# Layer 0's output stage in another order round tile 1, with the first expert group's 16 U rows gathered and multiplied in it

## The reference, cut to what matters

```python
# end of the mLSTM mixer; hs = both scan directions, 4 heads of 256
hn = (hs - mu) * lax.rsqrt(var + NORM_EPS) * norm_w          # per head
y = (sigmoid(o) * hn) @ w_out
x = layer_norm(DEEPNORM_ALPHA * x + m[2] * y, ln_mix_g, ln_mix_b)
f = peer_ffn(modulate(x, m[3], m[4]), w_q, subkeys, u_tab, v_tab)
x = layer_norm(DEEPNORM_ALPHA * x + m[5] * f, ln_ffn_g, ln_ffn_b)

def block(xt):                                               # peer_ffn, 128 tokens
    qh = (xt @ w_q).reshape(128, 8, 2, 128)
    s = einsum('thpd,hpnd->thpn', qh, subkeys)
    v_top, i_top = top_k(s, 16)
    sc, pos = top_k(sums of the 16 x 16 pairs, 16)           # 16 experts of a head
    gate = softmax(sc)
    act = gelu(einsum('td,ted->te', xt, u_tab[eidx]))        # U row times token
    return einsum('te,ted->td', gate * act, v_tab[eidx])     # weighted sum of V rows
```

## Time and profile before

| | before |
|---|---|
| median of 3 runs | 4410.88 us |
| profiled execution: its span | 4409.3 us |
| its own time beside the span | not recorded; the span is 1.6 us below the median of the runs |
| mean granted TensorE clock | 0.931 of 2.4 GHz |
| TensorE busy | 3529.3 us, 80% |
| VectorE busy | 3058.1 us, 69% |
| ScalarE busy | 746.8 us, 17% |
| GpSimd busy | 2512.6 us, 57% |
| DMA moved | 1491.65 MB, mean 338 GB/s |
| of it the gathers (software queue) | 1342.34 MB, 77.3% of the 16 DMA engines' span |

### The profile page before, as it was taken

One profiled execution on the slowest core, in us unless ns is written; L12 is line 12 of the kernel. 1 busy time (PEld: TensorE's weight loads), 2 busy tenths in 40 slices (PEclk: granted clock), 3 DMA queues, 4 the chain that ended last, 5 costly groups with the idle time before them and its releaser, 6 DMA issues. The chain is left out here.

```text
span 4409.3 us, 41525 instructions
## 1 busy us (share of the span) xinstructions
PE 3529.3 (80%) x11702; PEld 1756.0 (40%) x11702; DVE 3058.1 (69%) x7280; ACT 746.8 (17%) x2088; POOL 2512.6 (57%) x2589
## 2 busy tenths in 40 slices
PE   5987768888888888877977675888888888788876
PEld 3456544334333434422445343333343333333332
DVE  2754578777777777776779467766676766676776
ACT  0011111111111111211024131111111111111221
POOL 0000017767677777776755103777777777777775
PEclk8988889999999999999987787999999999999999
DMA  6731329999999999999987634999999999999998
GB/s 241 252 133 19 110 83 403 405 407 407 398 404 405 399 406 404 401 404 381 371 331 246 209 115 184 408 407 405 405 404 405 401 406 405 401 404 405 402 409 345
DMA packets 453089, 1491.65 MB, mean 338 GB/s; under 512 B 49860, under 2 KB 71236, under 8 KB 452612
## 3 DMA queue, kind: packets, MB, share of 16 engines
q0 software_dynamic: 368640, 1342.34, 77.3%
q1 hardware_dynamic: 80068, 138.34, 9.3%
q10 hardware_dynamic: 4160, 8.39, 0.6%
HBM read 1484.07 MB, written 4.82 MB: 338 GB/s over the span
## 5 line engine op out<-in xcount | busy, mean ns | idle before, releaser
L1629 DVE SCALAR_TENSOR_TENSOR wrk<-wrk,ps 128x1024 f32<-128x1024 f32 x1184 | 1439.9, 1218 | 801.8 <-DMA wrk<-in_peer_u,route_gate 801.2
L1567 POOL DMA_INDIRECT wrk<-in_peer_u,route_gate x1184 | 1124.8, 950 | 729.9 <-issue 458.3
L1431 PE MATMUL ps<-mod,diag 128*128 128x512 f32 x1152 | 568.4, 618 | 153.5 <-DMA mod<-in_peer_v,route_gate 153.2
L1576 POOL DMA_INDIRECT mod<-in_peer_v,route_gate x584 | 567.7, 972 | 178.5 <-issue 158.8
L1431 PE MATMUL ps<-mod,y 128*128 128x512 f32 x1184 | 530.3, 597 | 16.8 <-DMA mod<-in_peer_v,route_gate 16.8
L1431 PE MATMUL ps<-lnw,y 128*128 128x512 f32 x592 | 343.6, 735 | 223.7 <-ACT y L1505 222.7
L1431 PEld LDWEIGHTS ps<-mod,diag 128*128 128x128 f32 x1152 | 197.6, 189 | 516.4 <-DMA mod<-in_peer_v,route_gate 369.2
L1576 POOL DMA_INDIRECT lnw<-in_peer_v,route_gate x292 | 278.1, 952 | 210.9 <-DVE route_gate L1156 121.9
L1431 PE MATMUL ps<-big,diag 128*128 128x512 f32 x576 | 285.5, 618 | 100.5 <-DMA big<-in_peer_v,route_gate 100.5
L1431 PEld LDWEIGHTS ps<-mod,y 128*128 128x128 f32 x1184 | 217.8, 191 | 279.8 <-issue 222.2
L1576 POOL DMA_INDIRECT big<-in_peer_v,route_gate x292 | 276.1, 946 | 89.1 <-issue 73.2
(11 more groups left out here) (517 smaller groups left out, 4291.7 us busy)
## 6 DMA issues: line engine op xcount, KB each, us to landing
wrk<-in_gla_w_in SPq DMA_DIRECT2D x12, 2048.0 KB, 13.1
wrk<-in_peer_u,route_gate POOLq DMA_INDIRECT x1184, 9.3
big<-in_peer_w_q SPq DMA_DIRECT2D x16, 1024.0 KB, 16.7
mod<-modulation_rows SPq DMA_DIRECT2D x22, 512.0 KB, 6.6
lnw<-in_ada_w SPq DMA_DIRECT2D x14, 768.0 KB, 6.0
mod<-in_ada_w SPq DMA_DIRECT2D x40, 256.0 KB, 3.2
qk<-in_ada_w SPq DMA_DIRECT2D x13, 768.0 KB
mod<-in_ada_w SPq DMA_DIRECT2D x13, 768.0 KB, 6.1
```

The source lines that it names most:

```text
L1431: mm = pe.matmul(m.ps[:, b + h, :], diag[r], ring_v[r % RV][:, h * HALF:(h + 1) * HALF], start=r == 0 and i % 2 == 0, stop=r == on_pe(i) - ...
L1567: pool.indirect_dma_start(ring_u[r % RU], None, u, bass.IndirectOffsetOnAxis(ap=expert_slot(m, slot_at[work[i]])[:, r:r + 1], axis=0)).the ...
L1576: pool.indirect_dma_start(ring_v[r % RV], None, v, bass.IndirectOffsetOnAxis(ap=expert_slot(m, slot_at[work[i]])[:, r:r + 1], axis=0)).the ...
L1629: dve.scalar_tensor_tensor(out=ring_u[r % RU], in0=ring_u[r % RU], scalar=1.0, in1=xm_ps, op0=ALU.mult, op1=ALU.mult, accum_out=act_u[i % ...
```

## The change

In `mixer_output`:
- Both halves of w_out are loaded before the modulation and layer norm rows. `output(0, 1)` follows `output(0, 0)` directly.
- `head_norm` writes alternately into `m.y` and `m.diag`, so it waits for the transpose of two tiles before.
- VectorE does three head norms, then tile 1's residual (straight from PSUM) and `prepare`, head norm 3, the routing of group 0, head norm 4, then 16 dots of group 0 with the 14 pieces of group 1's routing between them, and last the four other residuals. TensorE does tile 1's queries and scores as soon as it can, in the middle of `output(1, 1)`.
- The other four products are copied by ScalarE from PSUM to `wrk` rows (`keep`), and their residuals read them there.
- GpSimd gathers the 16 U rows of group 0 in this stage, into a ring of 6 buffers (`Lead`).

In `peer`, layer 0: no U rows and dots of group 0. VectorE prepares the four tiles and starts `period(0)`. GpSimd starts with V rows of group 0 and U rows of group 1 in turn. In both layers: the V ring has 9 rows (five early ones, `big` 12, 13, 14, 5 and `wrk` 13, and four of `mod`), the second layer norm's rows go to `lnw`, and the scaling of X by ALPHA is done by ScalarE (`scale_tile`, five multiplications behind `copy_xT(4)`). `late` is an empty list in both layers, so what hangs on it does nothing.

```diff
@@ mixer_output @@
+    y = [m.y[:], m.diag[:]]
...
-            sp.dma_start(W[:, :, 0:HALF], w[:, :, 0:HALF]).then_inc(w_loaded[0], 16)
+            for n in range(2):
+                sp.dma_start(W[:, :, n * HALF:(n + 1) * HALF], w[:, :, n * HALF:(n + 1) * HALF]).then_inc(w_loaded[n], 16)
             load_rows(sp, m, a, layer, 0, (2,), "mix", loaded)
-            sp.dma_start(W[:, :, HALF:D], w[:, :, HALF:D]).then_inc(w_loaded[1], 16)
...
+        @block.gpsimd
+        def _(pool):
+            pool.wait_ge(head.sem, head.at(3, "gated"))
+            pool.sem_inc(lead.gather_passed, 1)
+            pool.wait_ge(front.route.sem, front.route.at(0, "expert"))
+            lead.gather(pool, u)
...
+            def keep(k):
+                act.wait_ge(product, k + 1)
+                act.copy(product_row(m, order[k]), pair_at(out_bank[k % 2])).then_inc(kept, 1)
...
+            front.copy_queries(act)
             front.copy_scores(act, 0)
             front.copy_scores(act, 1)
+            lead.show(act, front.act_scores)
+            keep(1)
             front.exp(act, 0)
+            evacuate(3)
+            sqrt_head(4)
+            keep(2)
             evacuate(4)
             front.exp(act, 1)
+            keep(3)
+            layer_norm_sqrt(act, m, rest, rest_act, 1)
+            layer_norm_sqrt(act, m, rest, rest_act, 2)
+            keep(4)
...
-                if k > 0:
-                    dve.wait_ge(transposed, k)
+                if k > 1:
+                    dve.wait_ge(transposed, k - 1)
...
+            head_norm(3)
+            for k in range(14):
+                front.route_piece(dve, passed, 0, k)
             head_norm(4)
-            front.routes(dve, passed)
-            residual(3)
-            residual(4)
+            pieces = route_one()
+            for r in range(TOPK):
+                lead.dot(dve, passed, r)
+                next(pieces, None)
+            for k in range(1, N):
+                dve.wait_ge(kept, k)
+                if k > 1:
+                    dve.wait_ge(rest.sem, rest.at(k - 1, "done"))
+                for _ in residual_steps(dve, m, rest, rest_act, k, order[k], product_row(m, order[k]), passed):
+                    pass
@@ peer @@
-    ring_v = [m.lnw[:, 0], m.lnw[:, 1], row_of(m.big, 14), row_of(m.big, 5)] + \
-             [m.mod[:, n, c, :] for n in range(2) for c in range(2)]
+    v_early = [row_of(m.big, 12), row_of(m.big, 13), row_of(m.big, 14), row_of(m.big, 5), row_of(m.wrk, 13)]
+    v_more = [m.mod[:, n, c, :] for n in range(2) for c in range(2)]
+    V_OPENS = len(late) * TOPK if late else len(v_early)
...
+            for n in range(2 if late else NT):
+                scale_tile(n)
...
             def row_u(i, r):
-                if i >= 1 or r >= RU:
+                if (i - U0) * TOPK + r >= RU:
                     pool.wait_ge(used_u, i * TOPK + r + 1 - RU)
...
             routed(0)
+            if lead:
+                routed(1)
+                for r in range(len(v_early)):
+                    row_v(0, r)
+                    row_u(1, r)
+                for r in range(len(v_early), RU):
+                    row_u(1, r)
+                for r in range(len(v_early), TOPK):
+                    row_v(0, r)
+                    if r + RU - len(v_early) < TOPK:
+                        row_u(1, r + RU - len(v_early))
...
-                if r >= 4 and r % 2 == 0 and r < 4 + 2 * NT:
...
-                    dve.tensor_scalar(m.X[:, t, :], m.X[:, t, :], ALPHA, None, ALU.mult).then_inc(summed, 1)
```

More of the change, by code:

```diff
@@ L10 @@
 from contextlib import ExitStack
+from itertools import chain
 import numpy as np
@@ L997, in _ @@
+            layer_norm(dve, m, rest, rest_act, 0, z, m.X[:, 1, :], "added", passed)
             dve.wait_ge(rest.sem, rest.at(0, "done"))
             front.prepare(dve)
-            head_norm(2)
-            residual(1)
             head_norm(3)
-            residual(2)
+            for k in range(14):
+                front.route_piece(dve, passed, 0, k)
             head_norm(4)
-            front.routes(dve, passed)
-            residual(3)
-            residual(4)
-def load_rows(sp, m, a, layer, first, which, ln, sem, rows=None):
+            pieces = route_one()
@@ L1011, in load_rows @@
+            for r in range(TOPK):
+                lead.dot(dve, passed, r)
[5 more added lines that the diff above has]
+                for _ in residual_steps(dve, m, rest, rest_act, k, order[k], product_row(m, order[k]), passed):
+                    pass
+def load_rows(sp, m, a, layer, first, which, ln, sem):
     for n in which:
@@ L1262, in routes, with __init__, peer @@
             for k in range(14):
-                routing_step(dve, self.m, self.b, self.layer, self.route, self.act_scores, self.act_exp, passed, R, R, k)
-def peer(nc, m, a, layer):
+                self.route_piece(dve, passed, R, k)
+class Ring:
+    def __init__(self, early, more, opens, total):
+        self.rows = early + more
+        free, self.slot, self.landing, self.after = list(range(len(early))), [], [], []
+        times, user = [0] * len(self.rows), [None] * len(self.rows)
+        for g in range(total):
+            if g == opens:
+                free = list(range(len(early), len(self.rows))) + free
+            n = free.pop(0)
+            free.append(n)
+            times[n] += 1
+            self.slot.append(n)
+            self.landing.append(times[n] * 16)
+            self.after.append(user[n])
+            user[n] = g
+def peer(nc, m, a, layer, lead=None):
     RU = RV = 8
+    U0 = 1 if lead else 0
     HALF_ROWS = TOPK // 2
@@ L1354, in _ @@
         def _(sp):
-            load_rows(sp, m, a, layer, 3, (2,), "ffn", rows_in, ln_rows)
+            for c in (1, 0):
+                if late:
+                    sp.wait_ge(rest.sem, rest.at(1 if c else 2, "scaled"))
+                sp.dma_start(m.mod[:, 2, c, :], a["rows"][layer, c, 5 * D:6 * D].partition_broadcast(P))\
+                    .then_inc(gate_in[c], 16)
+            if late:
+                sp.wait_ge(rest.sem, rest.at(len(late) - 1, "done"))
+            for n, name in enumerate(("g", "b")):
+                sp.dma_start(m.lnw[:, n, :], a[f"ln_ffn_{name}"][layer].partition_broadcast(P)).then_inc(ln_in, 16)
             for n in range(1, EH // 2):
@@ L1514, in group @@
                     layer_norm_sqrt(act, m, fin, fin_act, finished.index(tile(i - 2)))
+                if late and i == 0:
+                    copy_queries(2)
+                    copy_scores(2)
+                    layer_norm_sqrt(act, m, rest, rest_act, 0)
                 if len(now) == 2:
@@ L1693, in modulate_next, with route_steps, late_steps @@
                 dve.tensor_tensor(y, y, next_mod[0], ALU.add).then_inc(next_ready, 1)
+            def route_steps(R, first=0):
+                for k in range(first, 14):
+                    route_piece(R, k)
+                    yield
+            def late_steps(j):
+                t = late[j]
+                if j > 0:
+                    dve.wait_ge(rest.sem, rest.at(j - 1, "done"))
+                yield from residual_steps(dve, m, rest, rest_act, j, t, product_row(m, t), passed)
+                prepare(order.index(t))
+                yield
             def period(i):
```

342 lines of the change are left out of this document (203 added, 139 removed).

## The result

| | before | after |
|---|---|---|
| median (lowest to highest, runs) | 4410.43 us (4408.67 to 4413.34, 4) | 4387.49 us (4385.79 to 4388.14, 4) |
| ratio, 95% interval | | 0.9946 [0.9932, 0.996] |
| span of the profiled execution | 4409.3 us | 4385.7 us |
| mean granted clock | 0.931 | 0.933 |

The changed kernel is 22.9 us faster; 4391 was forecast. A second session with other executions gave 4392.3 us (4390.85 to 4394.56, 5 runs), ratio 0.9961 [0.9947, 0.9975] (`again_after`). First the head of its page, with busy time by engine and the GB/s of the 40 slices.

A forecast was written before the change was run, and what follows sets the result against it. DMA bound the expert stage's steady part, while VectorE ended the output stage with DMA share 0.26. Output stage +2.9, expert start -22, layer 1 -1.2 make -20.3: span 4409.3 becomes 4389.0, median 4391 us (range 4384 to 4403).

The forecast's parts named there:

- What bounds the kernel: Expert stage's steady part: DMA full, share 1.02, 1.3 us a row; output stage: VectorE ends it, DMA share 0.26.
- A: Output stage: with new order, 16 dots and their waits, it ends 2.9 us later; ends 8 us either way.
- B: Start of layer 0's expert stage: 16 rows already done, so 22 us less; 17 to 24 possible.
- C: Layer 1's expert stage: scalings off VectorE let group 0's last U row come earlier, 1.2 us less; 0 to 3.4.
- The sum: Whole kernel: A, B and C together -20.3 us, giving 4391 us; chance 0.62 for 4386 to 4396.
- 1: Rival, expert stage's first groups: TensorE's start sets them and V buffers hold GpSimd up; gain 13 us, 4398; chance 0.14.
- 2: Rival, output stage: dots wait for their rows, 5 to 10 us longer, 4396 to 4401; chance 0.08.
- 3: Rival: more comes back, B at 24, C at 3.4, output stage no longer; 4384; chance 0.08.
- 4: Rival, output stage: TensorE stays at the lower clock, stage ends 44 us late; 4432; chance 0.04.
- 5: Rival: the moved rows buy nothing, as something else sets the gathers' pace; 4408 to 4414; chance 0.04.
- those for "right": Output stage 1-6 us later; two idle times; no dot waits; GpSimd pause; 33rd row +27; DMA near 400; steady rates unchanged.
- those for "wrong": Idle times at the dots, granted clock near 0.5 between 530 and 600, GpSimd waiting for sums, steady rate not 403 GB/s.

The follow-up runs named there:

- rows_only: Kernel before, old output-stage order kept, with the 16 gathers and dots put in its second routing and the expert stage as changed: 4410.59 us, ratio 1.0004.
- experiment 5: Changed kernel with VectorE doing the five scalings of X again in layer 1 only: 4392.62 us, ratio 0.9955 to the kernel before.
- experiment 4: Changed kernel with 8 V buffers, as before, instead of 9: 4389.41 us, ratio 0.9954 to the kernel before.
- experiment 6: Changed kernel with 2 buffers instead of 6 for the output stage's 16 U rows: 4410.63 us, ratio 1.0001 to the kernel before.
- ring2: The kernel of experiment 6: changed kernel with 2 buffers, not 6, for the output stage's U rows; 4410.63 us.

## Why the prediction was right, step by step

- **What bounds the kernel.** Right. `rows_only` shows the exchange in pure form: 22.7 us more in the output stage, for dots and for the landing of the first rows, against 22.6 us less in the expert stage.
- **A, the output stage, +2.9.** The steps came in their order, the size was off: -0.2, in the second profile +0.7. From the stage's start product 1 was 0.8 us earlier (+26.5 for +27.3), the square root's wait 0.8 shorter, dots and routing took 26.25 us, not 27.9, and the residuals 32.9 for 32.8. Together 3.1 us. About 1.1 of it is that a routing between dots costs 8.0 us (26.25 less 16 dots of 1.14), where alone it costs 9.1. The landing, allowed 9.7 us, was 5.4 to 5.7, so the ring of six never held VectorE up. The low end, 8 us earlier with no idle time, leaves out the wait for product 1; without the three waits of 6.4, 7.6 and 3.2 us the sum comes to 14 us earlier.
- **B, the start of the expert stage, -22.** Right: -21.8 and -21.2. Of the two ways of working it out, the one by issue times (21.2) stood nearer than the one by bytes (23.5). The latter took 409 GB/s from +21 on, where 374 were measured: 14.9 MB by +41 and not 15.5, so 17.2 rows more than before, not 18.3, and 22.1 us. So nearly all of B is the 16 rows themselves, 20.6 us at 1.285.
- **C, layer 1, -1.2.** Wrong. The V row came 1.5 us earlier than with the old scalings (experiment 5), the stage stayed within 1.1 us of the old, to the longer side. The step that failed is "1.2 us earlier" taken as 1.2 us less. The ninth buffer, set at nothing here, seems worth up to 2 us at the start of layer 0 (experiment 4); B's 14 rows rest on it already.
- **The sum, -20.3.** By the stages' own lengths A and B gave -22.0 and -20.5 in the two profiles of the changed kernel (forecast -19.1), with layer 1 -21.8 and -19.5. What is left between these and the medians (-22.9 and -16.4 in the two sessions) is the size of the chance in unchanged code. That the sum came so near is partly luck: A put the cost 2.2 to 3.1 us too high, C the gain 1.4 to 2.3 too high, and the two cancel for the most part.
- **Rivals.** 1 fell: TensorE's sums start at +22.5, and GpSimd waits for them 0.3 us at most in the first 120 us of the stage. 2 did not act: no dot waited; experiment 6 shows the price it would have had. 3 is half there: the stage got no longer, but B stood at 22 and not 24. 4 fell: the half products took 7.03 to 7.13 us and the queries 7.41 at the new places. 5 fell: the expert stage gave back 21.1 to 22.6 us for the 16 rows.
- **The signs.** Two of those for "right" did not come. VectorE's last row of the output stage ended 2.1 us earlier than before, at 631.61, and not 1 to 6 later (A's miss and the start's 1.9). And the DMA rate was not near 400 from +3 on: 236 GB/s from +3 to +6, 403 to 414 from there to the pause, then the dip to 320. The others came: the two idle times, no DMA wait at the dots, the pause, the 33rd row, the steady 403. None of those for "wrong" was seen.

## What to carry to other kernels

Moving work between stages pays by the difference of what bounds them: the same 16 rows were worth nothing where their dots lengthened the stage by 22.7 us, and 7 to 9 us where the order hid part of their cost behind waits and they lengthened it by 13. Ask of the same move in both directions: after DMA bytes went into the VectorE-bound stage, VectorE's residuals went the other way for another 18 to 19 us. And size a term of 2 us by the length of the stage it acts in, not by the total, while unchanged code moves by 3 to 8 us by chance.

## What the runs showed of the hardware

- A gather of 512 KB landed 4.4 us after its issue from a ring of two buffers, 5.4 to 5.7 from a ring of six (medians). The first of the kernel before, with eight issued back to back beside plain loads, took 9.7 to the dot behind it. A landing read under load is a poor guide to an empty queue.
- With 14 gathers issued one behind the other ahead of it, a pause of 4.6 us in their issue cost 1.3 rows of the flow, not 3.5 (4.6 / 1.3).
- TensorE's granted clock over the output stage was 0.83 with the new order (129 us), and in the two kernels whose stage lasts 152 us 0.79 with the old order (`rows_only`) and 0.78 with the new (`ring2`): so the order alone doesn't set this mean. In `ring2` TensorE has nothing to do from 603 us on, and the mean clock from there to 654 us is 0.52. Its first transposes in the changed kernel after 9.38 us of idle time took 1.97 us for eight, later ones 1.04.
